# First channel tile's preparation moved beside the last projection tiles, and the modulation's first groups moved forward

## The reference

```python
def trunk_layer(...):
    mod = jax.nn.silu(c) @ mod_w + mod_b              # modulation, 6 x 2048 columns
    mod_c = jax.nn.silu(c_ctx) @ mod_w + mod_b
    sh1, sc1, g1, sh2, sc2, g2 = jnp.split(mod[:, None, :], 6, axis=-1)
    h = modulate(rms_norm_2(x, norm1_w), sh1, sc1)
    hc = modulate(rms_norm_2(ctx, norm1_w), csh1, csc1)
    p = h @ in_w                                      # projections
    pc = hc @ (in_w[:, :A_COLS + B_COLS] if last else in_w)
    ya, ya_c = rwkv7_branch(...)                      # branch A, 16 heads of 64
    yb, yb_c = gdn_branch(...)                        # branch B, 8 heads of 128
    x = x + g1 * merge_branches(ya, yb, pg, up_a, up_b, out_w)
    x = x + g2 * squared_relu_mlp(modulate(rms_norm_2(x, norm2_w), sh2, sc2), mlp_w1, mlp_w2)

def rwkv7_prepare(z, w0, w_up, a0, a_up, k_k, k_a):
    kk = l2_normalize(heads(k * k_k))
    tw = jnp.tanh(xw)
    for d in range(2):                                # two directions
        w = -jax.nn.softplus(-(w0[d] + tw @ w_up[d])) - 0.5
        a = jax.nn.sigmoid(a0[d] + xa @ a_up[d])
        k_d = k * (1.0 + (a - 1.0) * k_a)
        dirs.append((heads(jnp.exp(-jnp.exp(w))), heads(k_d), heads(a) * kk))

def rwkv7_scan(...):                                  # along the tokens
    sa = jnp.einsum('bhvk,bhk->bhv', s, kk_t)
    s = s * dec_t - sa[..., None] * b_t + v_t[..., None] * k_t
```

## Time and profile before

| what | value |
|---|---|
| median of three runs | 3752.62 us |
| the profiled execution, its own time | 3750.07 us |
| its span, first to last instruction | 3748.3 us |
| mean granted TensorE clock | 0.977 |
| TensorE busy | 3575.6 us, 95% |
| VectorE busy | 2195.2 us, 59% |
| ScalarE busy | 1522.8 us, 41% |
| GpSimd busy | 1648.5 us, 44% |
| addition of tile 0, of tile 91 (L2621) | 1156.01, 1887.35 us |
| first instruction of the convolution | 1902.13 us |

### The profile page before, as it was taken

The page is one execution under the profiler, slowest core; times in us unless marked ns, Lnnn a source line. Parts: engine busy times, 40 slices in busy tenths (PEclk is TensorE's granted clock), DMA queues, the critical chain, the costliest instruction groups (busy, mean ns, idle before and its releaser), DMA issues. The chain is left out here.

```text
span 3748.3 us, 80553 instructions
## 1 busy us (share of the span) xinstructions
PE 3575.6 (95%) x34272; PEld 3122.4 (83%) x34272; DVE 2195.2 (59%) x4040; ACT 1522.8 (41%) x2753; POOL 1648.5 (44%) x1195
## 2 busy tenths in 40 slices
PE   7999998999997999999979999999989999999998
PEld 6888787888786888888868888888879898989897
DVE  5645535655536776777756677666656654544443
ACT  4444434444434432332323334343334453535343
POOL 5555455555554543333321111111116566666664
PEclk9999999999999999999979999999989999999999
DMA  6445554444354777678610100000016445554453
GB/s 234 180 169 191 187 197 158 175 180 185 137 188 159 261 268 258 243 260 294 239 32 25 29 29 29 25 24 16 3 58 237 180 179 186 181 185 189 183 182 133
DMA packets 116373, 586.92 MB, mean 157 GB/s; under 512 B 20912, under 2 KB 40368, under 8 KB 51376
## 3 DMA queue, kind: packets, MB, share of 16 engines
q1 hardware_dynamic: 116016, 581.76, 42.6%
HBM read 561.00 MB, written 20.71 MB: 155 GB/s over the span
## 5 line engine op out<-in xcount | busy, mean ns | idle before, releaser
L582 PE MATMUL bank<-act_L,part_L 128*128 128x512 f32 (+1 forms) x4864 | 932.8, 347 | 8.8 <-DMA cst<-in_cst 4.8
L582 PEld LDWEIGHTS bank<-act_L,part_L 128*128 128x128 f32 x4864 | 755.4, 191 | 144.6 <-issue 28.1
L582 PE MATMUL bank<-act_P,part_P 128*128 128x512 f32 (+1 forms) x3488 | 716.0, 365 | 17.9 <-POOL part_P L3255 12.9
L3255 POOL TENSOR_TENSOR part_C<-wring,part_C 128x512 fp32r<-128x512 f32 x320 | 567.1, 1781 | 362.4 <-ACT part_C L1447 362.4
L3255 POOL TENSOR_TENSOR part_L<-wring,part_L 128x512 fp32r<-128x512 f32 x304 | 526.2, 1732 | 442.9 <-ACT part_L L1447 434.8
L582 PEld LDWEIGHTS bank<-act_P,part_P 128*128 128x128 f32 x3488 | 590.6, 189 | 136.6 <-DVE arena_P L2621 16.2
L3255 POOL TENSOR_TENSOR part_P<-wring,part_P 128x512 fp32r<-128x512 f32 x184 | 306.3, 1670 | 427.8 <-ACT part_P L1447 427.8
L1447 ACT ACTIVATE part_C<-wring 128x1024 fp32r<-128x1024 f32 x320 | 338.0, 1057 | 346.7 <-PE bank L582 343.7
L582 PE MATMUL bank<-act_Y,part_C 128*128 128x258 f32 (+1 forms) x3840 | 464.2, 283 | 9.4 <-POOL part_C L3255 9.4
L582 PEld LDWEIGHTS bank<-act_Y,part_C 128*128 128x128 f32 x3840 | 463.3, 191 | 9.8 <-issue 9.6
L582 PE MATMUL bank<-arena_B 64*64 64x64 f32 (+2 forms) x11200 | 440.5, 235 | 30.9 <-ACT arena_B L1447 8.5
(11 more groups left out here) (266 smaller groups left out, 3727.5 us busy)
## 6 DMA issues: line engine op xcount, KB each, us to landing
wring<-in_w SPq DMA_DIRECT2D x404, 1024.0 KB, 4.8
arena_P<-in_w SPq DMA_DIRECT2D x64, 1024.0 KB, 5.3
mring<-in_w SPq DMA_DIRECT2D x32, 1024.0 KB, 6.8
z_kept<-arena_P SPq DMA_DIRECT2D x34, 256.0 KB, 5.7
z_kept<-arena_P SPq DMA_DIRECT2D x58, 128.0 KB, 6.0
xT<-z_kept SPq DMA_DIRECT2D x26, 256.0 KB, 2.6
arena_C<-z_kept SPq DMA_DIRECT2D x32, 128.0 KB, 2.9
cst<-z_kept SPq DMA_DIRECT2D x24, 128.0 KB, 2.1
```

The source lines that it names most:

```text
L582: return e.matmul(out, lhsT, rhs, start=start, stop=stop)
L3255: e.tensor_tensor(wl[:, 4:8, :], wring[s % NS][:, 8 * j + 4:8 * j + 8, :], wh[:, 4:8, :].bitcast(F32), sub).then_inc(*mark("pool_lo", "lop ...
```

## The change

The preparation of channel tile 0 for the first direction is issued in stage P, right after `base_a_tile(0)`, on TensorE, ScalarE and VectorE, with banks of that stage's ring (`NR`). The buffers that it writes are taken from the region "mid", which the modulation's sums hold until then. So it waits for the last sum (`modsum`, 23), and the modulation's list is shortened at its head: its first two groups have gaps of 12 and 4 tiles instead of 16 and 8. At the beginning of stage B the convolution of branch B is no longer held back (`FIRST_B` 4 to 0), and the streams skip `prep` there for tile 0 and direction 0. The wait for the last four stores of stage P moves from the first direction's preparation to the second's.

```diff
+            before_b = ("mid",)
+            R.a, R.cc, R.e1, R.e2 = [alloc(512, before_b) for _ in range(4)]
+            R.pr = alloc(256, before_b)
...
-                kb_ = alloc(1024)
+                kb_ = alloc(1024, rest_b if d else before_b)
...
-                g.KK, g.Kt, g.Bt, g.RK, g.RB = [alloc(512) for _ in range(5)]
+                g.KK, g.Rd, g.es = [alloc(n, rest_b if d else before_b) for n in (512, 256, 8)]
+                g.Kt, g.Bt, g.RK, g.RB = [alloc(512) for _ in range(4)]
...
-        MODP = [(8, 16), (9, 8)] + [(n, 4) for n in range(10, 24)]
+        MODP = [(8, 12), (9, 4)] + [(n, 4) for n in range(10, 24)]
...
-        LATE_A, LATE_B, LATE_TA, LATE_TB, FIRST_B = 2, 3, 0, 0, 4
+        LATE_A, LATE_B, LATE_TA, LATE_TB, FIRST_B = 2, 3, 0, 0, 0
...
@@ -1820 @@ (ScalarE; VectorE the same, TensorE without the wait)
                 yield from weave.until(("ptile", 84))
                 yield from base_a_tile(0)
+                w.wait_ge(done("modsum", 23))
+                yield from prep(0, 0, NR)
...
-            def prep(c, d):
-                g, ring = R.d[d], DR[d]
+            def prep(c, d, ring):
+                g = R.d[d]
...
                 if d == 0:
-                    for n in range(NPR - 4, NPR):
-                        w.wait_ge(done("zs", n))
                     w.wait_ge(done("bon", c - 1)) if c else None
                     tt(R.pr, R.rrk, e1[:, 0:256], mult).then_inc(*mark(V))
                 else:
+                    for n in range(NPR - 4, NPR):
+                        w.wait_ge(done("zs", n))
                     tt(R.tp, R.rrk, e1[:, 0:256], mult).then_inc(*mark(V))
...
-                    yield from prep(c, d)
-                    weave.said.add(("prep", c, d))
+                    if c or d:
+                        yield from prep(c, d, DR[d])
+                        weave.said.add(("prep", c, d))
+                    else:
+                        yield
...
@@ -3404 @@ (GpSimd)
-                    for _ in range(5):
+                    for _ in range(5 if c or d else 1):
                         yield
```

More of the change, by code:

```diff
@@ L413, in program @@
             R.rrk = alloc(256, ("top",))
-            R.pr, R.bon, R.tp, R.s, R.bv, R.gate = [alloc(256, ("stores",)) for _ in range(6)]
+            R.bon, R.tp, R.s, R.bv, R.gate = [alloc(256, ("stores",)) for _ in range(5)]
             D.zr, D.sr = [D.Z["k"], D.Z["v"]], [D.S["k"], D.S["v"]]
             R.d = []
+            before_b = ("mid",)
+            R.a, R.cc, R.e1, R.e2 = [alloc(512, before_b) for _ in range(4)]
+            R.pr = alloc(256, before_b)
+            rest_b = ("parts", "h", "mid", "w0", "w1", "w2", "xT", "cst", "wa2", "top", "made", "stores")
             for d in range(2):
                 g = Mem()
-                kb_ = alloc(1024)
+                kb_ = alloc(1024, rest_b if d else before_b)
                 g.Kd, g.Bd = g.X, g.XP = kb_[:, 0:512], kb_[:, 512:1024]
                 g.NA, g.AK, g.XT = alloc(1024), alloc(1024), alloc(1024)
-                g.KK, g.Kt, g.Bt, g.RK, g.RB = [alloc(512) for _ in range(5)]
+                g.KK, g.Rd, g.es = [alloc(n, rest_b if d else before_b) for n in (512, 256, 8)]
+                g.Kt, g.Bt, g.RK, g.RB = [alloc(512) for _ in range(4)]
                 g.Q = [alloc(512) for _ in range(2)]
@@ L425, in program @@
             R.lo = lo_.rearrange("p (j c) -> p j c", j=6)
-            R.a, R.cc, R.e1, R.e2 = [alloc(512) for _ in range(4)]
             R.Vt = [x.rearrange("p (q c) -> p q c", q=4) for x in R.Vt]
@@ L443, in program @@
             for g in R.d:
-                g.Y, g.Rd = alloc(256, ("stores",)), alloc(256)
+                g.Y = alloc(256, ("stores",))
             for g in R.d:
@@ L448, in program @@
                 g.S, g.R, g.U = [alloc(128) for _ in range(3)]
-            for g in R.d:
-                g.es = alloc(8)
         with ExitStack() as st:
```

## The result

| | kernel before | changed kernel |
|---|---|---|
| median of 11 runs | 3752.72 us (3750.9 to 3754.66) | 3762.76 us (3759.42 to 3776.69) |
| ratio | | 1.0036, 95% interval 1.0029 to 1.0044 |
| span of the profiled execution | 3748.3 us | 3759.7 us |
| mean granted clock | 0.977 | 0.976 |

The changed kernel is slower by 10.0 us, by the medians. The ratio is close to that of the means (3765.7 against 3752.7 us), on which the three runs above 3774 us weigh. The forecast was no change (3752.6 us). 3762.8 lies at the very edge of its range for 8 in 10 (3743 to 3763), outside the 3746 to 3759 of the forecast itself, and on the side to which it gave 0.19.

The account below looks back on a forecast made before the run. TensorE was taken as busy nearly throughout, paced by a VectorE-ScalarE loop in narrow tiles and idle at the recurrence entry; +8.1 + 0.8 - 1.9 + 1.9 + 0.5 - 9.4 = 0.0 gave 3752.6 us, range 3746 to 3759 (8 in 10: 3743 to 3763).

Parts of the forecast that it names:

- The loop of VectorE and ScalarE: Narrow projection tiles: the two engines' cycle sets the pace, 7.16 us a tile with four modulation rows in tiles 23 to 31.
- The products: Tile 86: the moved preparation's two products now stand in the TensorE stream that bounds, +1.9 us (0 to +2.0).
- The column sums in the tail: Two column sums fewer where TensorE is the bound, 0.95 us each, -1.9 us (0 to -1.9).
- The entry: Start of the recurrence: VectorE's preparation ahead of the convolution goes, -9.4 us (-12.8 to -8.4).
- the 1.0 that the prediction had put down for one slow instruction alone: Recurrence entry: one instruction slowed beside clearing, 1.0 us allowed to stay out of the 10.44 us removed.
- Rival 1: Nine narrow tiles: modulation weight stripes come late, 8.2 us a tile, +9.4, time 3762 us; chance 0.13.
- Rival 3: Recurrence entry: nothing is given back because a later wait doesn't move, +9.4 kept, time 3762 us; chance 0.06.
- By my count it comes about when TensorE wants it: Tile 87: the low split for tile 89, queued behind eight preparation instructions, comes about in time, +0.5 us (0 to +3).
- weighed it for 4.2 us: Recurrence entry: GpSimd's six set-up copies could each shut out a convolution instruction for 0.7 us, 4.2 us lost.
- the front: Narrow tiles 23 to 31, four modulation rows each: +8.1 us (+3.1 to +23).
- the +0.8 allowed for in tiles 11 to 22: Sixteen modulation rows instead of twelve there: some 0.4 us lost in two tiles, +0.8 us (0 to 1.6).

Follow-up runs that it names:

- e3: Changed kernel with first gaps 8 and 8 and the schedule one round earlier, so tiles 11 to 26 carry two rows each; 3757.51 us.
- e6: e5 with three gap-8 groups at the head, preparation from tile 88, its last eight VectorE instructions held back 5 rounds instead of 13; 3738.41 us.
- e9: Kernel before with only the modulation's schedule of e6, preparation and convolution at their old places; 3746.07 us.
- e2: Changed kernel with the last eight VectorE instructions of the moved preparation 13 rounds later, behind the last low split of the projections; 3758.26 us.
- e7: Changed kernel with the eight VectorE preparation instructions in two groups of four, the low split for tile 89 between them; 3755.38 us.
- e4: Changed kernel with each group's column sum and its addition two rounds later; 3759.28 us.
- e8: The changed kernel itself again, for a second profile and more times; 3764.56 us.
- e1: Kernel before with only the changed kernel's modulation list (first gaps 12 and 4); 3762.59 us.
- e5: Changed kernel with the edits of e2, e3 and e4 together; 3745.49 us.
- e10: The kernel of e6 a second time, with more runs; 3739.71 us.

## Why the prediction was wrong

**Where it held.** The loop of VectorE and ScalarE: 7.16 us forecast, 7.11 to 7.14 measured in tiles 24 to 30 (tile 27: 6.82; 23 and 31: 6.9), and e3, e6 and e9 show that a row behind the addition is free. The products: +1.9 and +1.7. The column sums in the tail: -1.9 and -1.8. The entry: -9.4 and -9.4, but that the sizes agree is luck in part. The convolution came 9.9 us nearer to the last addition and not 10.44, mostly since the clearing began 0.4 us later. From the convolution's first instruction to the scores' products it takes 0.5 us more. Together that is the 1.0 that the prediction had put down for one slow instruction alone. The one instruction that lost 0.94 us (1.43 above, 0.49 before) began 0.55 us ahead of the products, which waited for ScalarE's evacuation and not for it. Rival 1 (stripes late) did not come: 324 GB/s were moved, more than the 311 that it was priced with, at 7.12 us a tile. Rival 3 (nothing given back at the entry) gave 3762, the time that was measured, but by a cause that isn't there; so did rival 1.

**The step that failed: "By my count it comes about when TensorE wants it. +0.5 (0 to +3...)".** It measured +6.8. Three things were wrong in it. First the length of the queue. At the durations of their kind alone, 0.5 for the first and 0.4 to 0.7 for the others, the eight take about 5 us; they took 9.7, since five GpSimd splits fall beside them (three and one in the rows, and one more). The prediction had the rows of that effect in hand for the modulation's rows (1.78 us beside a split, 0.74 otherwise) and did not apply them here. e2 shows the same instructions at 0.69 us without GpSimd. Second, what waits behind the queue: not the low split alone but also the addition of tile 87, which frees the bank for tile 89 and by the trace came last. Third the price of being late: bounded at 3 us, "one narrow tile's half late", without the clock. A pause of 4.59 us was followed by half clock, which cost 2.2 more; one of 1.19 in e7 was not.
The Trainium skill, "SBUF — State Buffer", section "SBUF: two separate sides", has the rule for the first: a VectorE instruction with two SBUF inputs and a GpSimd instruction that reads SBUF shut each other out. In the tail this case's trace agrees (1.78 against 0.68 us). At the entry, where the prediction weighed it for 4.2 us, one instruction with two SBUF inputs lost 0.2 us beside a copy (L3053, 0.71 against 0.48). The 0.94 us were lost by a TENSOR_SCALAR with one such input beside a clearing, which is not what this rule speaks of.

**The term that was mis-sized: the front.** Tiles 23 to 32 cost +10.2, and +11.8 in the four other profiles with this schedule, against +8.1. VectorE's loop itself cost less than forecast, +7.5 against +8.7, and the +0.8 allowed for in tiles 11 to 22 was 0.3 at most. The column sums were taken as 0.95 us of TensorE, hidden in tiles of 7.16. That they wait for VectorE's last row, and that one of them lies where the narrow tiles end, was left out. That the clock falls behind such a wait, where TensorE is the bound, was left out too. e4 took the wait away, and with it the fall: 2.1 us less than in the first profile, 3.7 less than in the others, 3.5 by the median.

**What the sum missed.** The same ledger with its two failures taken out gives 11.3 - 6.8 - 2.1 = 2.4, of which 1.0 lies ahead of the change and 3.4 in the recurrence: the rest, -2.0, is within some 2 us of the forecast of 0.0. It is the ledger of one pair of executions, and in the other one of the changed kernel (e8) the projections were 3.6 us longer, mostly by the clock.

**What stays open.** The changed kernel's runs spread over 17 us (25 with e8), those of the kernel before over 4 to 6. e1, with the schedule alone, has six runs over 15 us, so the spread needs no moved preparation. The runs of these two kernels above 3774 us have a mean granted clock of 0.970 to 0.973, those below 3765 us 0.974 to 0.977. In the one late execution that was profiled (e2, 3768.8), three channel tiles in a row are 112.6 to 112.7 us long instead of 109, at a mean clock of 0.94 instead of 0.97. What makes an execution fall into that was not found; of e3's and e4's 22 runs none was later than 3763.4, but e5 and e10, with the same edits, had runs at 3765.5 and 3753.9. An estimate from the two recurrences (1846.6 and 1844.1 us, before 1843.2): some 1 to 3 of the changed kernel's 10 us can't be given to a place. Open too is why e9's median gained 6.1 us where its ledger, without the stretch of half clock at 1655 us, gives 4.2 ahead of the recurrence.

## What to carry to other kernels

Work moved under a cover costs its queue time: find every instruction behind it that someone waits for (here a low split, and an addition that frees a bank), add up what stands ahead of it at the durations that hold beside the other engines at that place, and compare this with how far the consumer's stock reaches. Here the cover was ample (14.66 us of an idle VectorE ahead of tile 91's addition) and the place was wrong by 13 rounds. In a loop of two engines, look for the gap in which one waits for the other: what stands there is free, and the same work one position on costs 0.63 to 0.65 us. And a semaphore wait of a fast engine for a slow engine's last item (the column sums) belongs late in the consumer's queue.

## What the runs showed of the hardware

What TensorE did before its granted clock fell to half in the projections, and before it stayed at full:

| before | clock | profiles |
|---|---|---|
| pause of 4.59 us ahead of tile 89 | half | changed kernel, e3, e4, e8 |
| pause of 3.80 us at a column sum | half | e3 |
| pause of 2.86 to 2.88 us at a column sum | half | changed kernel, e1, e2, e7, e8 |
| pause of 1.78 to 1.96 us at a column sum | half | e1, e2, e7, e8 |
| pause of 1.71 us at the same column sum | full | changed kernel |
| pause of 1.19 us ahead of tile 89 | full | e7 |
| pause of 1.40 to 1.52 us near 1209 us | full | all twelve |
| pauses of about 0.3 and 0.7 us in every tile | full | e4 |
| no pause, 24 short products (2.75 us in e4) | half in eight, full in four | all twelve |

The same fall can cost nothing or its full price. At 1330, where VectorE sets the pace at 7.12 us a tile, it cost nothing; at 1360, where TensorE is the bound, it cost 1.6 us, by the changed kernel's second profile against the first, which had no fall there. In the recurrence, stretches of half clock fall at other places from one execution to the next, and a channel tile takes from 108.4 to 113.4 us by them. A difference of 3 to 4 us between two profiled executions of this kernel, in the projections as in the recurrence, is by itself no evidence of a cause in the code.
